# A two-layer decoder on one core: mLSTM output by token tile, a diagonal in the final norm, and sample steps and weight slabs in another order

## The chip, the cores and the metric

The kernel runs as one program on one core of a Trainium2 chip. The metric is the device time of one execution in microseconds (us), less is better; several executions are timed and their median is given. Beside these, one execution is recorded by the hardware profiler: its span, every instruction on every engine, what each engine waited for, and the clock that TensorE was granted. The engines are called as in the profile: PE (matrix products), PEld (its weight loads), DVE (vector engine), ACT (scalar engine), POOL (GpSimd), SP (the queue that issues most DMAs).

## What is computed

Two decoder layers work on 512 prompt tokens (one causal sequence) and 8 sample tokens (one step each, with states of their own). A layer adds to the residual a mix of three branches (mLSTM, gated linear attention, pooling), then a channel mixer: dense SwiGLU in layer 0, a top-2-of-8 mixture of experts in layer 1. A last RMS norm follows. The parts that matter here:

```python
# mLSTM, one head, prompt: b = cumsum(log f), m_t the running maximum
s   = (q_t . k_s) * exp(b_t - b_s + i_s - m_t)          # causal weights
num = sum_s s * v_s + w_inter * (C q_t)
den = sum_s s       + w_inter * (n . q_t)
h   = num / max(|den|, exp(-m_t))
C_new, n_new = decayed state + sum_s w_s v_s k_s^T, ... # state returned
# sample tokens: the same with one token and a state C0, n0, m0 of each
# gated linear attention: S_t = diag(a_t) S_{t-1} + k_t^T v_t ; o_t = q_t S_t
# head norm, gates, projections, experts ...
y = x * rsqrt(mean(x^2) + eps) * final_norm_g
```

The prompt starts from zero states, so its inter terms vanish. All is float32.

## The kernel before

Every engine has its own instruction stream, written out by hand, and semaphores order them. Activations stand feature-major (features on the 128 partitions, 520 tokens along the free axis). A weight slab is 128 x 1024 float32; ACT rounds it into `w_hi` (`split_hi`, L756), DVE takes the rest into `w_lo` (`split_lo`, L1132), and PE makes three products per tile (line 1847). A slab costs PE 48 of these matmuls.

The mixers of a layer are chains of small steps over several engines. To keep PE busy during them, the 48 projection slabs of the layer (q, k, v, pooling input, gates) are cut into 96 half slabs, and each engine's stream has calls `fill(k)` between its chain steps. On PE `fill` is k half slabs of products. On ACT every even half slab is a `split_hi` two slabs ahead. On DVE every even half slab (L1426) is a `split_lo` two slabs ahead and `fill_out` (L1440), which takes the result of the slab before from PSUM, so that PE may use that bank again. All engines count the same half slabs. Since each stream is strictly in order, a DVE that waits in a chain step also holds the splits queued behind it.

Order in a layer: `inputs`, `gla`, `gla_decode` (the 8 sample states of the gated linear attention, two groups `j`), `mlstm_columns`, `mlstm` (4 heads), `mlstm_decode` (8 sample states, 4 heads with two buffers), `head_norm`, gates and merge.

mLSTM, one head on PE (L1947): transposes of k and v and a broadcast of `row_M`, `fill(2)`, scores of key tiles 0 and 1, `fill(1)`, scores of 2 and 3, `fill(1)`, then the output group, `fill(2)`, a wait for `h`, the pooling products, `fill(1)`. The output group makes the numerator feature-major in PSUM bank 6 (`vt` as weights, `wgt` moving, 512 + 384 + 256 + 128 columns), the denominator in bank 7 on all partitions (`ones` as weights, the same columns), exp(-m) broadcast to bank 4 (`row_f`, 512 columns), the new state from `vw` and `kt`, and its `n` row. After the group ACT copies state and row out and takes the absolute value of the 128x512 denominator (L885), DVE takes the maximum with bank 4 (L1363), the reciprocal (L1365) and the product with the numerator (L1367, the step `h`), then does its `fill(3)`. The even halves fall so that in heads 0 and 2 the half slab that PE does right after the pooling products needs the first `fill_out` of this `fill(3)`; in heads 1 and 3 it doesn't.

POOL does the pooling averages (`pool_average`, L575), one per head, with elementwise instructions on 128x512 tiles, and issues the DMAs of states. After the last head it stores C, n and m, waits until these stores have landed (their memory is used again), loads the sample states and rows (`Cs`, `kb`, `qb`), waits for `sample_norms`, and sends its result through memory (`den_rows`) to all partitions (`rec_b`).

`mlstm_decode` on DVE (L1396): `fill(2)`, the same wait for the stores, `sample_norms` (L1371, nine steps on 8 partitions), then per head `Cs` times its factor, `kb` times its factor, `fill(2)`, their sum, the product with `qb`, `fill(2)`, a reduction and the product with `rec_b`. `gla_decode` on DVE (L1245): `fill(4)`, then the two products and the sum for group `j`, on which PE waits after a `fill(4)` of its own.

The end: after the last expert pass POOL stores the last outputs (`store_y`), waits for them in `stored` (L739: a wait on a register's value, a one-element POOL operation, a wait for that), and gathers each token's second row (`rows_back`, L726, five tiles). For each tile DVE adds it (L1784), ACT squares and sums and takes the root (L1084, L1087), DVE the reciprocal (L1789), ACT scales the 128x1024 tile (L1092), PE transposes it in 8 blocks (L2227) into one of two PSUM pairs, DVE multiplies by the gain (L1794), SP stores it.

Of the kernel before, what the change touches and what calls it, by code (L numbers as in the profile page):

```python
# [152 lines left out]
def decoder(nc, slabs, x_in, vectors, if_bias, gate_w, pool_w, consts, ml_m0, ml_n0, ml_C0,  # L153
# [7 lines left out]
    def sem(name):  # L161
# [54 lines left out]
    acol = sb("acol", [P, TT, H], where=early)  # L216
    w3 = sb("w3", [H, 3, NS_TOK], where=early)
# [34 lines left out]
    vt = sb("vt", [P, TT, P], where=ml_mem)  # L252
    wgt = sb("wgt", [P, TT, NP_TOK], where=ml_mem)
    dm = sb("dm", [P, TT, P], where=ml_mem)
    den = sb("den", [P, NP_TOK], where=ml_mem)
    den2 = sb("den2", [P, NP_TOK], where=ml_mem)
# [115 lines left out]

    rows = Steps(sem("rows"), gates=2, abs=2, exp=1, ln=1, logf=1, b=1, a=1, M=1, m=2, enm=1,
                 inter=1, smax=1, sdiff=3, sexp=1, turn=1, turned=4)
# [48 lines left out]
    second_in = [sem(f"second_in{i}") for i in range(5)]  # L423
    low_added, both_added = sem("low_added"), sem("both_added")
# [59 lines left out]

    def gathered_rest():

        return ps[:, 2:4, P:2 * P].rearrange("p a (b c) -> p a b c", c=REST)
# [9 lines left out]
    def pair(i):  # L497

        return 6 if i % 2 == 0 else 2

# [65 lines left out]
    def _(pool):  # L566
# [33 lines left out]
        for l in range(DEPTH):  # L600
# [33 lines left out]
            for h in range(H):  # L634
                pool_average(l, h)
                i = H * l + h
                pool.wait_ge(ml.sem, ml.after("cst", i))
                pool.dma_start(C_p[l, h], C_t[:, h]).then_inc(st_C, 16)
            pool.dma_start(n_p[l], n_row[:]).then_inc(st_nm, 16)
# [13 lines left out]
            for h in range(2):  # L653
# [3 lines left out]
            pool.wait_ge(sn.sem, sn.after("drec", l))  # L657
            pool.dma_start(den_rows[l, 0].rearrange("(b h) -> b h", h=H), den8[:, 2]).then_inc(den_stored, 16)
            pool.wait_ge(den_stored, 16 * (l + 1))
            pool.dma_start(rec_b[:].rearrange("p b h -> p (b h)"),  # L660
                           den_rows[l].to_broadcast([P, NS_TOK * H])).then_inc(rec_in, 16)
            pool.dma_start(n_s[l], n_s0[:]).then_inc(st_ns, 16)
# [56 lines left out]
        def store_y(j):  # L719

            pool.wait_ge(y_main, j + 2)
            pool.dma_start(slots[bass.ds(j * CAP, P)], yt[:, 0]).then_inc(y_stored, 16)
            pool.wait_ge(y_added, j + 2)
            pool.dma_start(slots[bass.ds(j * CAP + P, REST)], yt[0:REST, 1]).then_inc(y_stored, 16)
# [8 lines left out]
        with pool.Fori(0, last) as j:  # L733
            pool.wait_ge(gathered, j * 2 + 2)
            load_rows(j * CAP + CAP)
            store_y(j)
# [12 lines left out]
        store_y(last)  # L749
        stored(last * 32 + 48, 2)  # L750
# [4 lines left out]
    def _(act):  # L755
# [103 lines left out]
        def mlstm(l):  # L859
# [4 lines left out]
            for h in range(H):  # L864
# [20 lines left out]
                nc.scalar.activation(den[:], ps[:, 7], ACT.Abs).then_inc(ml.sem, 1)  # L885
# [192 lines left out]
        def last_norm():  # L1078

            for i in range(6):  # L1080
                if i < 5:
                    rws = slice(0, tile_rows(i))
                    act.wait_ge(both_added, i + 1)
                    nc.scalar.activation(rows_in[rws], xt[rws, i], ACT.Square,  # L1084
                                         accum_out=ssq[rws, i:i + 1]).then_inc(fin_sq, 1)
                    act.wait_ge(fin_sq, i + 1)
                    nc.scalar.activation(rst[rws, i:i + 1], ssq[rws, i:i + 1], ACT.Sqrt, bias=eps[rws],  # L1087
                                         scale=1.0 / D).then_inc(fin_root, 1)
                if i > 0:
                    rws = slice(0, tile_rows(i - 1))  # L1090
                    act.wait_ge(fin_rs, i)
                    nc.scalar.activation(xt[rws, i - 1], xt[rws, i - 1], ACT.Copy,  # L1092
                                         scale=rst[rws, i - 1:i]).then_inc(fin_scaled, 1)
# [33 lines left out]
    def _(dve):  # L1127
# [117 lines left out]
        def gla_decode(l):  # L1245

            for j in range(2):
# [5 lines left out]
                fill(4)  # L1253
# [5 lines left out]
                inc(tt_op(Ss[:, j], Ss[:, j], vb[:, j], ALU.add))  # L1259
                at("o")  # L1260
# [63 lines left out]
        def mlstm_columns(l):  # L1324
# [4 lines left out]
            inc(nc.vector.tensor_copy(acol[:], ps[:, 4, 0:16].rearrange("p (a h) -> p a h", h=H)))  # L1329
            inc(nc.vector.tensor_copy(w3t[:], ps[0:NS_TOK, 4, 32:44].rearrange("p (a h) -> p a h", h=H)))  # L1330
# [5 lines left out]
        def mlstm(l):  # L1336
            for h in range(H):
                rep = H * l + h
# [3 lines left out]
                inc(nc.vector.tensor_copy(vt[:], ps[:, 5].rearrange("p (a d) -> p a d", d=P)))  # L1342
# [17 lines left out]
                inc(tt_op(vw[:], vt[:], wcol[:].unsqueeze(2).to_broadcast([P, TT, P]), ALU.mult))  # L1360
# [35 lines left out]
        def mlstm_decode(l):  # L1396
# [3 lines left out]
            sample_norms(l)  # L1400
            for h in range(H):
# [10 lines left out]
                fill(2)  # L1412
# [357 lines left out]
        def last_norm():  # L1770
# [8 lines left out]
            for i in range(7):  # L1779
# [10 lines left out]
                if i > 1:  # L1790
                    rws = tile_rows(i - 2)
                    dve.wait_ge(fin_turned, i - 1)
                    b = pair(i - 2)
                    tt_op(x[:, :, P * (i - 2):P * (i - 2) + rws],  # L1794
# [41 lines left out]
    def _(pe):  # L1836
# [110 lines left out]
        def mlstm(l):  # L1947
# [21 lines left out]
            for h in range(H):  # L1969
                rep = H * l + h  # L1970
                at = lambda name: pe.wait_ge(ml.sem, ml.after(name, rep))
                if h > 0:
                    pe.wait_ge(po.sem, po.after(f"y{h - 1}", l))
# [392 lines left out]
```

## Time and profile before

| | us |
|---|---|
| median of 3 timed runs | 2181.29 (2179.46 to 2182.74) |
| the profiled execution, its own time | 2184.47 |
| its span, first to last instruction | 2182.8 |
| PE busy | 2073.6 (95%) |
| DVE busy | 1335.9 (61%) |
| ACT busy | 847.2 (39%) |
| POOL busy | 209.2 (10%) |

The time outside the span is 1.7 us. A row of a timeline has start, duration, engine, line, operation, output from inputs, shapes and count; in square brackets stands how long the engine was idle before it and what ended that.
### The profile page before, as it was taken

What the parts mean: (1) busy time and instruction counts of PE and PEld (TensorE: products, weight loads), DVE (VectorE), ACT (ScalarE), POOL (GpSimd) and SP (SyncE); (2) the same over time, 40 slices, a digit from 0 to 9 for tenths busy, and PEclk for the clock granted to TensorE, in tenths of its full rate; (3) what the DMA queues carried; (4) which work ended last, traced back from release to release, by engine and by line L of the source; (5) the groups of instructions that cost most, each with busy time, mean ns of one, the idle gap of its engine ahead of it and who ended that gap; (6) DMA issues with size and microseconds to landing.
All of it is one profiled execution on the core that took longest, in us unless ns stands there. A gap on an engine that the chain in (4) does not pass through costs nothing.

```text
span 2182.8 us, 38536 instructions
## 1 busy us (share of the span) xinstructions
PE 2073.6 (95%) x15443; PEld 1945.9 (89%) x15443; DVE 1335.9 (61%) x1964; ACT 847.2 (39%) x1175; POOL 209.2 (10%) x344
## 2 busy tenths in 40 slices
PE   7999999999999999999999999995999999999994
PEld 7998889999999999999988899994888888888873
DVE  5554457665555542345543666655788787888876
ACT  4311222543433222234122225433455555555644
POOL 0002231010000000000022310102000000000011
PEclk9999999999999999999999999997999999999996
DMA  4232238557222232222422384633677777787775
GB/s 177 81 116 84 91 103 283 171 180 282 93 89 96 87 97 93 92 88 79 119 86 79 128 278 151 189 99 120 214 241 243 239 249 247 225 262 238 241 263 165
DMA packets 108637, 352.37 MB, mean 161 GB/s; under 512 B 14168, under 2 KB 18328, under 8 KB 108248
## 3 DMA queue, kind: packets, MB, share of 16 engines
q1 hardware_dynamic: 87464, 278.46, 39.6%
q0 software_dynamic: 21056, 72.21, 10.0%
q8 instruction: 91, 1.49, 0.3%
q14 instruction: 26, 0.21, 0.0%
HBM read 304.80 MB, written 46.27 MB: 161 GB/s over the span
## 4 chain that ended last, share of the span: by engine, by line
PE 66%; DVE 14%; issue 7%; DMA 6%; ACT 6%; POOL 1%; ACTq 0%; SPq 0%; DVEq 0%; POOLq 0%
PE ps L1847 52%; PE ps L1841 7%; DVE w_lo L1135 6%; ACT w_hi L761 4%; DMA raw<-slabs 4%; PE ps L2151 3%; DVE gsum L1726 1%; PE ps L2153 1%; DVE usum L1737 1%; PE ps L2165 1%; DVE ma_parts L1767 1%; PE ps L2171 1%; DVE den L1365 1%; DVE yt L1762 0%; DMA mlstm_reciprocals<-den 0%
## 5 line engine op out<-in xcount | busy, mean ns | idle before, releaser
L1135 DVE TENSOR_TENSOR w_lo<-raw,w_hi 128x1024 fp32r<-128x1024 f32 x487 | 601.2, 1235 | 306.0 <-ACT w_hi L761 303.7
L761 ACT ACTIVATE w_hi<-raw 128x1024 fp32r<-128x1024 f32 x488 | 508.9, 1051 | 440.9 <-PE ps L1847 393.4
L1847 PE MATMUL ps<-h_hi,w_hi 128*128 128x260 f32 x2544 | 526.8, 288 | 21.7 <-DVE h_lo L1144 13.6
L1847 PE MATMUL ps<-h_hi,w_lo 128*128 128x260 f32 x2544 | 514.6, 284 | 0.0
L1847 PE MATMUL ps<-h_lo,w_hi 128*128 128x260 f32 x2544 | 513.9, 284 | 0.0
L1847 PEld LDWEIGHTS ps<-h_hi,w_hi 128*128 128x128 f32 x2544 | 396.9, 190 | 36.7 <-DVE w_lo L1135 22.0
L1847 PEld LDWEIGHTS ps<-h_hi,w_lo 128*128 128x128 f32 x2544 | 394.4, 189 | 0.0
L1847 PEld LDWEIGHTS ps<-h_lo,w_hi 128*128 128x128 f32 x2544 | 394.2, 190 | 0.0
L2151 PE MATMUL ps<-hg,w_hi 128*128 128x320 f32 x1408 | 375.3, 349 | 16.2 <-DVE w_lo L1135 12.9
L2153 PE MATMUL ps<-hg,w_lo 128*128 128x160 f32 x1408 | 334.8, 238 | 0.0
L2151 PEld LDWEIGHTS ps<-hg,w_hi 128*128 128x128 f32 x1408 | 266.2, 189 | 36.1 <-DVE w_lo L1135 24.0
L2153 PEld LDWEIGHTS ps<-hg,w_lo 128*128 128x128 f32 x1408 | 270.5, 192 | 2.0
L2165 PE MATMUL ps<-w_hi,ma_parts 128*128 128x512 f32 x352 | 115.5, 409 | 9.7 <-DVE w_lo L1135 9.0
L1056 ACT ACTIVATE msig<-gsum 128x160 f32<-128x160 f32 x88 | 29.5, 336 | 145.8 <-DVE gsum L1726 145.8
L2165 PEld LDWEIGHTS ps<-w_hi,ma_parts 128*128 128x128 f32 x352 | 59.3, 188 | 20.6 <-issue 10.7
L1847 PE MATMUL ps<-br_lo,w_hi 128*128 128x260 f32 x384 | 77.3, 283 | 0.0
L1847 PE MATMUL ps<-br_hi,w_hi 128*128 128x260 f32 x384 | 77.1, 282 | 0.0
L1847 PE MATMUL ps<-br_hi,w_lo 128*128 128x260 f32 x384 | 77.0, 282 | 0.0
L1847 PE MATMUL ps<-a_hi,w_hi 128*128 128x260 f32 x352 | 71.0, 283 | 0.0
L1847 PE MATMUL ps<-a_hi,w_lo 128*128 128x260 f32 x352 | 70.8, 282 | 0.0
L1847 PE MATMUL ps<-a_lo,w_hi 128*128 128x260 f32 x352 | 70.6, 282 | 0.0
L1064 ACT ACTIVATE ma_parts<-ma 128x160 fp32r<-128x160 f32 x88 | 29.7, 337 | 82.7 <-DVE ma L1739 82.4
(362 smaller groups left out, 2595.0 us busy)
## 6 DMA issues: line engine op xcount, KB each, us to landing
raw<-slabs SPq DMA_DIRECT2D x489, 512.0 KB, 4.2
gates_kept<-sq SPq DMA_DIRECT2D x64, 260.0 KB, 2.2
gs<-gates_kept POOLq DMA_DIRECT2D x64, 260.0 KB, 3.6
token_slots<-zeros POOLq DMA_DIRECT2D x1, 9600.0 KB, 34.7
rows_in<-token_slots POOLq DMA_DIRECT2D x9, 512.0 KB, 4.4
Cs<-ml_C POOLq DMA_DIRECT2D x8, 512.0 KB, 6.8
kb<-mlstm_key_query_rows POOLq DMA_DIRECT2D x8, 512.0 KB, 6.7
qb<-mlstm_key_query_rows POOLq DMA_DIRECT2D x8, 512.0 KB, 8.2
```

The lines of the kernel that those rows point to most:

```text
L761: nc.scalar.activation(w_hi[:, n % SPL], raw[:, place(n)], ACT.Copy).then_inc(hi_ready, 1)
L1056: nc.scalar.activation(msig[:], gsum[:], ACT.Sigmoid).then_inc(m_sig, 1)
L1064: nc.scalar.activation(ma_parts[:, f % 2, 0:CAP], ma[:, f % 2], ACT.Copy).then_inc(m_hi, 1)
L1135: tt_op(w_lo[:, n % SPL], raw[:, place(n)], w_hi[:, n % SPL].bitcast(F32), ALU.subtract).then_inc(lo_ready, 1)
L1365: inc(nc.vector.reciprocal(den2[:], den[:]))
L1726: nc.vector.tensor_reduce(gsum[:], addends(b), AX.X, ALU.add).then_inc(m_sum, 1)
L1737: nc.vector.tensor_reduce(usum[:], addends(b + 1), AX.X, ALU.add).then_inc(m_up, 1)
L1841: return mm(out, a, b, start=start, stop=stop, skip_group_check=True)
L1847: ins = mm(out[:, hf], wgt_part[:, slot, tile], in_part[:, kk, HALF * hf:HALF * (hf + 1)], start=first and not ends and in_part is in_hi, ...
L2151: mm(out[:, 0:2 * CAP], w_hi[:, (s0 + s) % SPL, kk], hg[:, kk], start=kk == 0, stop=False, skip_group_check=True)
L2153: ins = mm(out[:, 0:CAP], w_lo[:, (s0 + s) % SPL, kk], hg[:, kk, 0:CAP], start=False, stop=kk == KT - 1, skip_group_check=True)
L2165: mm(ps[:, 4 + hf_], parts[:, at:at + P], w[:, slot_n, 4 * hf_:4 * hf_ + 4], start=f == 0 and a == 0, stop=f == FE_TILES - 1 and a == 2)
```

## The change

Four edits:

- mLSTM output. `vt` has a 129th column of ones. For each query tile the weights `wgt` are the stationary operand and `vt` with its ones the moving one: 10 matmuls of 129 columns give numerator and denominator with tokens on partitions. The products with `ones` and the broadcast of `row_f` go; exp(-m) comes as columns (`fcol`) from four more small transposes before the heads. Absolute value, maximum and reciprocal are on 128x4; ACT scales each of the four query tiles into `out_rows`, PE transposes them back into bank 6 (the step `back`), DVE copies to `br`. On PE `back` stands where the wait for `h` was; the next head waits for `h`.
- Samples. `sample_norms` is called in the DVE stream ahead of head 1; POOL sends its result after head 1 and fetches it after head 2.
- Slabs. In `gla_decode` one slab of DVE's `fill` goes from ahead of each state to behind its sum; in `mlstm_decode` one goes from inside head 0 to ahead of it.
- The end. DVE makes a diagonal matrix of the reciprocal roots; PE multiplies each tile by it (float32 matmuls in place of transposes), so ACT's scaling goes; four PSUM pairs in place of two; DVE's product with the gain comes one turn later. The last stores have a semaphore of their own and are waited for directly.

```diff
     ml = Steps(sem("mlstm"), ...
-               vw=1, out=1, cst=2, absd=1, maxd=1, rec=1, h=1)
+               vw=1, out=1, cst=2, absd=1, maxd=1, rec=1,
+               scaled=TT, back=1, h=1)
 # POOL, head loop
                 pool.dma_start(C_p[l, h], C_t[:, h]).then_inc(st_C, 16)
+                if h == 1:
+                    pool.wait_ge(sn.sem, sn.after("drec", l))
+                    pool.dma_start(den_rows[l, 0]..., den8[:, 2]).then_inc(den_stored, 16)
+                    pool.dma_start(n_s[l], n_s0[:]).then_inc(st_ns, 16)
+                if h == 2:
+                    pool.wait_ge(den_stored, 16 * (l + 1))
+                    pool.dma_start(rec_b..., den_rows[l]...).then_inc(rec_in, 16)
 # POOL, end
-        store_y(last)
-        stored(last * 32 + 48, 2)
+        store_y(last, last_stored)
+        pool.wait_ge(last_stored, 32)
 # ACT, mlstm
-                nc.scalar.activation(den[:], ps[:, 7], ACT.Abs).then_inc(ml.sem, 1)
+                nc.scalar.activation(den[:]..., out_sums(), ACT.Abs).then_inc(ml.sem, 1)
+                at("rec")
+                for tt in range(TT):
+                    c = (P + 1) * (tt % 2)
+                    nc.scalar.activation(out_rows[:, tt], ps[:, 6 + tt // 2, c:c + P], ACT.Copy,
+                                         scale=den[:, tt:tt + 1]).then_inc(ml.sem, 1)
                 fill(2)
 # ACT, last_norm
-                    nc.scalar.activation(xt[rws, i - 1], xt[rws, i - 1], ACT.Copy,
-                                         scale=rst[rws, i - 1:i]).then_inc(fin_scaled, 1)
 # DVE, gla_decode
-                fill(4)
+                fill(2)
 ...
                 inc(tt_op(Ss[:, j], Ss[:, j], vb[:, j], ALU.add))
+                fill(2)
                 at("o")
 # DVE, mlstm
             for h in range(H):
+                if h == 1:
+                    sample_norms(l)
 ...
-                inc(tt_op(den[:], den[:], ps[:, 4], ALU.max))
+                inc(tt_op(den[:], den[:], fcol[:, :, h], ALU.max))
                 at("maxd")
-                inc(nc.vector.reciprocal(den2[:], den[:]))
-                at("rec")
-                inc(tt_op(br[:, h, 0:NP_TOK], ps[:, 6], den2[:], ALU.mult))
+                inc(nc.vector.reciprocal(den[:], den[:]))
+                at("back")
+                inc(nc.vector.tensor_copy(br[:, h, 0:NP_TOK], ps[:, 6]))
                 fill(3)
 # DVE, mlstm_decode
-            sample_norms(l)
+            fill(2)
 ...
                 inc(by_token(kb[:, b], vs8[:, h]))
-                fill(2)
+                if h > 0:
+                    fill(2)
 # DVE, last_norm
+                    dve.wait_ge(fin_rs, i)
+                    ts_op(root_diag(i - 1), ident[rws, rws], rst[rws, i - 1:i], None, ALU.mult).then_inc(
+                        fin_scaled, 1)
 # PE, mlstm
                 if h > 0:
                     pe.wait_ge(po.sem, po.after(f"y{h - 1}", l))
+                    pe.wait_ge(ml.sem, ml.after("h", rep - 1))
 ...
                 for tt in range(TT):
-                    exact(ps[:, 6, tt * P:], vt[:, tt], wgt[:, tt, tt * P:], tt == 0, tt == TT - 1)
-                for tt in range(TT):
-                    exact(ps[:, 7, tt * P:], ones, wgt[:, tt, tt * P:], tt == 0, tt == TT - 1)
-                exact(ps[:, 4], select[:, h], row_f[:, 0:NP_TOK])
+                    c = (P + 1) * (tt % 2)
+                    for ts in range(tt + 1):
+                        exact(ps[:, 6 + tt // 2, c:c + P + 1], wgt[:, ts, token_tile(tt)], vt[:, ts],
+                              ts == 0, ts == tt)
 ...
                 fill(2)
-                pe.wait_ge(ml.sem, ml.after("h", rep))
+                at("scaled")
+                for tt in range(TT):
+                    ins = nc.tensor.transpose(ps[:, 6, tt * P:(tt + 1) * P], out_rows[:, tt], ident)
+                ins.then_inc(ml.sem, 1)
 # PE, end
-            if i >= 2:
-                pe.wait_ge(fin_out, i - 1)
+            if i == 4:
+                pe.wait_ge(fin_out, 1)
             for kk in range(KT):
-                ins = nc.tensor.transpose(ps[:, pair(i) + kk // 4, ...], xt[...], ident[...])
+                ins = exact(ps[:, tail_pair(i) + kk // 4, ...], xt[...], root_diag(i))
```

## Rows read from the trace of the kernel before

**Rows 1.** The page, busy time of each engine over the span.
```profile
PE 2073.6 (95%) x15443; PEld 1945.9 (89%) x15443; DVE 1335.9 (61%) x1964; ACT 847.2 (39%) x1175; POOL 209.2 (10%) x344
```

**Rows 2.** Waits of PE, whole span: who waited for whom, total, times, longest.
```profile
PE ps L1847 <- DVE sq L1450: 6.7, 7, 2.1
PE ps L1841 <- DVE Ss L1259: 3.5, 4, 0.9
```

**Rows 3.** Timeline of PE in mLSTM head 0 of layer 0.
```profile
199.61 2.32 PE L1841 MATMUL ps<-wgt,vt 128*128 128x512 f32 x8
...
205.07 1.16 PE L1841 MATMUL ps<-kt,vw 128*128 128x128 f32 x8
...
207.12 0.51 PE L1847 MATMUL ps<-h_hi,w_hi 128*128 128x260 f32 x2
...
213.17 1.15 PE L1841 MATMUL ps<-pd,pw 128*128 128x260 f32 x4
215.00 0.47 PE L1847 MATMUL ps<-h_hi,w_hi 128*128 128x260 f32 x2 [0.69 <-DVE sq L1450]
```

**Rows 4.** Timeline of PE in the gated linear attention: matmuls of 128 columns.
```profile
136.73 0.39 PE L1841 MATMUL ps<-qz,S_in 128*128 128x128 f32 x2
136.95 0.39 PE L1841 MATMUL ps<-att,gvt 128*128 128x128 f32 x2
```

**Rows 5.** Timeline of ACT after the output group of head 0.
```profile
207.23 0.28 ACT L881 ACTIVATE C_t<-ps 128x128 f32<-128x128 f32 x1 [14.18 <-PE ps L1841]
```

**Rows 6.** Timeline of DVE, end of head 0 and begin of head 1, layer 0.
```profile
209.04 3.35 DVE L1365 RECIPROCAL den<-den 128x512 f32<-128x512 f32 x1
213.03 1.21 DVE L1135 TENSOR_TENSOR w_lo<-raw,w_hi 128x1024 fp32r<-128x1024 f32 x1
...
216.03 2.42 DVE L1135 TENSOR_TENSOR w_lo<-raw,w_hi 128x1024 fp32r<-128x1024 f32 x1 [1.17 <-ACT w_hi L761]
...
220.16 0.69 DVE L1342 COPY vt<-ps 128x512 f32<-128x512 f32 x1 [1.11 <-PE ps L1841]
...
224.01 0.17 DVE L1347 COPY wcol<-wgt 128x4 f32<-128x4 f32 x1 [2.43 <-ACT wgt L877]
```

**Rows 7.** Timeline of POOL at the begin of head 1, layer 0.
```profile
216.30 1.05 POOL L581 TENSOR_TENSOR pa<-br 128x511 f32<-128x511 f32 x1
217.41 1.07 POOL L582 COPY pa<-br 128x1 f32<-128x1 f32 x1
```

**Rows 8.** Timeline of DVE, begin of `mlstm_decode` in layer 0.
```profile
321.69 0.18 DVE L1377 TENSOR_TENSOR vs<-v,w3b 128x32 f32<-128x32 f32 x1
...
325.78 0.17 DVE L1394 RECIPROCAL den<-den 8x4 f32<-8x4 f32 x1
...
329.18 1.23 DVE L1266 TENSOR_TENSOR kb<-kb,vs 128x1024 f32<-128x1024 f32 x1
```

**Rows 9.** Busy time of engines by stretch, then PEclk, DMA share, GB/s.
```profile
1077.00:1078.00 1.00, 1.00 (x6) 1.00 (x6) 0.85 (x2) 0.00 (x0) 0.42 (x1) 0.50 0.02 8
```

**Rows 10.** Busy time of PE in a stretch of the routing, then PEclk.
```profile
1498.00:1498.50 0.50, 0.50 (x5) 0.50 0.00 0
```

**Rows 11.** Timeline of PE in the routing.
```profile
1495.85 4.49 PE L2106 MATMUL ps<-con,x 128*128 128x128 f32 x24
```

**Rows 12.** Timeline of POOL at the end: the wait for the last stores.
```profile
2151.85 1.86 POOL L742 TENSOR_TENSOR rst<-rst 1x1 f32<-1x1 f32 x1 [1.75 <-DMA token_slots<-yt]
2154.31 1.45 POOL L729 DMA_INDIRECT second<-token_slots,order  x1 [0.60 <-POOL rst L742]
```

**Rows 13.** Timeline of PE at the end.
```profile
2165.30 1.97 PE L2227 MATMUL ps<-con,xt 128*128 128x128 f32 x8 [21.34 <-ACT xt L1092]
```

**Rows 14.** Timeline of DVE at the end.
```profile
2161.41 1.28 DVE L1784 SCALAR_TENSOR_TENSOR xt<-second,share,xt 128x1024 f32<-128x1024 f32 x1 [1.05 <-DMA second<-token_slots,order]
...
2176.74 1.39 DVE L1794 TENSOR_TENSOR x<-ps,vec 128x1024 f32<-128x1024 f32 x2 [1.12 <-PE ps L2227]
```

**Rows 15.** One line's instructions: count, duration min, median, max.
```profile
L1229 DVE TENSOR_SCALAR S_in<-S,ge x16: 276/278/283, 105.9 to 1055.7; 128x128 f32<-128x128 f32 x16
```

More of the change, by code:

```diff
@@ L216, in decoder @@
     acol = sb("acol", [P, TT, H], where=early)
+    fcol = sb("fcol", [P, TT, H], where=early)
     w3 = sb("w3", [H, 3, NS_TOK], where=early)
@@ L251, in decoder @@
     kt = sb("kt", [P, TT, P], where=ml_mem)
-    vt = sb("vt", [P, TT, P], where=ml_mem)
+    vt = sb("vt", [P, TT, P + 1], where=ml_mem)
     wgt = sb("wgt", [P, TT, NP_TOK], where=ml_mem)
     dm = sb("dm", [P, TT, P], where=ml_mem)
-    den = sb("den", [P, NP_TOK], where=ml_mem)
-    den2 = sb("den2", [P, NP_TOK], where=ml_mem)
+    out_rows = sb("out_rows", [P, TT, P], where=ml_mem)
+    den = sb("den", [P, TT], where=ml_mem)
+    sb("beside_den", [P, NP_TOK - 4 * TT], where=ml_mem)
     vw = sb("vw", [P, TT, P], where=ml_mem)
@@ L499, in pair, with tail_pair, root_diag @@
         return 6 if i % 2 == 0 else 2
+    def tail_pair(i):
+        return (6, 2, 4, 0)[i % 4]
+    def root_diag(i):
+        return gain_row[0:tile_rows(i), P * i:P * i + tile_rows(i)]
     def gain_of(r):
@@ L656, in _ @@
                 across(qb, 1, h, qb_in)
[L657 to L662, printed above, removed]
             for h in range(H):
@@ L735, in _ @@
             load_rows(j * CAP + CAP)
-            store_y(j)
+            store_y(j, y_stored)
         pool.wait_ge(gathered, last * 2 + 2)
@@ L1078, in last_norm @@
         def last_norm():
[L1080 to L1091, printed above, removed]
-                    nc.scalar.activation(xt[rws, i - 1], xt[rws, i - 1], ACT.Copy,
-                                         scale=rst[rws, i - 1:i]).then_inc(fin_scaled, 1)
+            for i in range(5):
+                rws = slice(0, tile_rows(i))
+                act.wait_ge(both_added, i + 1)
+                nc.scalar.activation(rows_in[rws], xt[rws, i], ACT.Square,
+                                     accum_out=ssq[rws, i:i + 1]).then_inc(fin_sq, 1)
+                act.wait_ge(fin_sq, i + 1)
+                nc.scalar.activation(rst[rws, i:i + 1], ssq[rws, i:i + 1], ACT.Sqrt, bias=eps[rws],
+                                     scale=1.0 / D).then_inc(fin_root, 1)
         fills = [0, 0]
@@ L1329, in mlstm_columns @@
             inc(nc.vector.tensor_copy(acol[:], ps[:, 4, 0:16].rearrange("p (a h) -> p a h", h=H)))
+            inc(nc.vector.tensor_copy(fcol[:], ps[:, 4, 64:80].rearrange("p (a h) -> p a h", h=H)))
+            nc.vector.memset(vt[:, :, P:P + 1], 1.0).then_inc(ones_beside, 1)
             inc(nc.vector.tensor_copy(w3t[:], ps[0:NS_TOK, 4, 32:44].rearrange("p (a h) -> p a h", h=H)))
@@ L1778, in last_norm @@
                        ALU.add).then_inc(low_added, 1)
-            for i in range(7):
+            for i in range(8):
                 if i < 5:
@@ L1953, in mlstm @@
                                     ident[0:H, 0:H])
+                nc.tensor.transpose(ps[:, 4, 64 + H * tt:64 + H * tt + H], row_f[:, token_tile(tt)],
+                                    ident[0:H, 0:H])
             for a in range(3):
@@ L1973, in mlstm @@
                     pe.wait_ge(po.sem, po.after(f"y{h - 1}", l))
+                    pe.wait_ge(ml.sem, ml.after("h", rep - 1))
+                else:
+                    pe.wait_ge(ones_beside, l + 1)
                 for tt in range(TT):
@@ L2223, in _ @@
             pe.wait_ge(fin_scaled, i + 1)
-            if i >= 2:
-                pe.wait_ge(fin_out, i - 1)
+            if i == 4:
+                pe.wait_ge(fin_out, 1)
             for kk in range(KT):
-                ins = nc.tensor.transpose(ps[:, pair(i) + kk // 4, P * (kk % 4):P * (kk % 4) + rws],
-                                          xt[0:rws, i, P * kk:P * (kk + 1)], ident[0:rws, 0:rws])
+                ins = exact(ps[:, tail_pair(i) + kk // 4, P * (kk % 4):P * (kk % 4) + rws],
+                            xt[0:rws, i, P * kk:P * (kk + 1)], root_diag(i))
             ins.then_inc(fin_turned, 1)
```

31 lines of the change are left out of this document (20 added, 11 removed).

## The prediction

> **What bounds it now.** I read the busy times first: PE works 95% of the span [rows 1], so time is saved where PE gets less to do or where PE waits, and nowhere else. Then the waits of PE. Two of them are touched: PE waits 7 times, 6.7 us in all, for the DVE product that frees a PSUM bank (`fill_out`), and 4 times, 3.5 us, for the sum of a sample state in `gla_decode` [rows 2]. Of the 6.7, four are the 0.69 us after the pooling products in heads 0 and 2 of each layer [rows 3]; the other 3.9 lie in `mlstm_decode`. The timelines of one head (PE, ACT, DVE, POOL) show the rest: the output group runs from 199.61 to 207.12, its first three products until 205.07, so 5.46 us; the `fill(2)` behind it until about 213.1; and the reciprocal of 3.35 us [rows 6] ends with its neighbours just as this fill does, so it costs PE nothing today. Last, the end: PE idles 21.3 us and begins at 2165.30 [rows 13].
>
> **mLSTM heads.** The three products of 5.46 us become 10 matmuls of 128 by 129. Their price is not in the trace for this operand pair; the nearest rows are the 128-column matmuls of the gated attention, one start each 0.22 us [rows 4], and the four of the state, 1.16 us with their drain, 0.29 each [rows 3]. So 2.2 to 2.9 us, and the gain is 2.6 to 3.2 us; I take 2.9. Against it stand four transposes. The blocks of 8 in the routing give 4.49/24 = 0.19 us with the clock partly at half [rows 11]; I take 0.11 at the full clock, 0.45 us for four. The chain between, ACT's copies and absolute value, two tiny DVE steps and four scalings of some 0.28 us [rows 5], ends about 2.6 us after the group and is hidden by the 6 us of `fill(2)`; without this fill it would cost those 2.6 us. What is late next: DVE now waits for `back`, and its `fill(3)` is queued behind. Let F be the end of PE's `fill(2)`. Today DVE begins the split at 213.03 and PE starts its next half slab at 215.00, F + 1.9 [rows 3, 6]. Then: transposes to F + 0.65, DVE copy 0.6, and the same 1.97 from split to PE: F + 3.2. Heads 0 and 2 lose 1.3 us, heads 1 and 3, whose next half slab needs nothing of this, 0.5. Gain per layer 2 x (2.9 - 1.3) + 2 x (2.9 - 0.5) = 8.0; both layers 16.0 (13.6 to 18.4). The four small transposes, `fcol` and the column of ones ahead of the heads cost PE about 0.3 us per layer, an estimate below one 128-column matmul each [rows 4]: -0.6.
>
> **Sample norms ahead of head 1.** Nine DVE steps last from 321.69 to 325.95, 4.3 us [rows 8]. In the old place they stood before the load of `kb` had landed (329.18) and were nearly free. In the new place DVE comes out of head 0 at F + 6.5 (after the split that took 2.42 us in place of 1.21 [rows 6]), so the steps end at F + 10.8 if nothing disturbs them. Queued behind them is the `vt` copy, which PE's transposes allow at F + 8.1. From that copy to the `wcol` that PE waits for are 4.05 us [rows 6]; PE's own `fill(2)` covers until F + 14.0. So PE waits at least 0.85 us. But POOL begins its pooling average just here. The rows show both sides blocking: the split that doubled ran into POOL's addition, and POOL's one-column copy took 1.07 us while the split ran [rows 6, 7]. The six norm steps with two SBUF inputs that are long or early may each wait for one POOL step of 0.2 to 1.5 us, which puts the end at F + 14.7 and the wait at 4.7 us. The Trainium skill (SBUF - State Buffer, Who interferes with whom) states that a DVE instruction with two SBUF inputs and a POOL instruction that reads SBUF exclude each other for a whole instruction, while a reduction does not contend. Without such a lock the loss would be 0.85 us a layer, with it 4.7. By these rows [rows 6, 7] I take 4.0. A PE that idles 4 us then finds its clock at half; the trace has three such stretches after idle time or tiny matmuls, one of them at 1077 [rows 9] lasting from 1076 to 1083, the others (332 and 1304) about 3 to 4 us; at half the clock that is 1.5 us lost. Sum 2 x 5.5 = -11.0, bounds -1.7 to -13.
>
> **Slabs and decode.** With `rec_b` ready and one slab ahead, DVE no longer has a split queued behind the `kb` transfer (landed 329.18), and the 3.9 us of PE waits go. What is next is PE itself: two slabs of 5.8 us per head against 9.8 us of DVE work; the loads of the third and fourth state come just in time. +3.9, bounds 1 to 3.9. In `gla_decode` the sum comes one split and one `fill_out` (1.8 us) sooner, more than the 0.9 of each wait; only group 0 is bound by its transfer. Of 3.5 I take 2.8 (2.0 to 3.5). Two of the half-clock stretches, 1076 and 332, follow waits that go; they cost about 3.4 and 1.4 us. Such stretches can fall elsewhere, so I take half, 2.4 (0 to 4.8).
>
> **The end.** The one-element POOL operation takes 1.86 us and the gather starts 0.6 later, at 2154.31 [rows 12]. The direct wait gives back 1.2 (gathers then run beside DVE's additions) to 2.4; I take 1.7. Tile 0's scale is then ready after DVE's second addition (2161.41 + 1.2 - 1.7), a reciprocal and a diagonal of 0.28 us [rows 14, 15]: PE starts at 2161.5 in place of 2165.30. Its price rises: a tile took 1.97 us [rows 13], and 8 matmuls take 1.8 to 2.3 us at the full clock, 3.5 to 4.6 at half. The clock is at half after 21 us of idling. In the routing PE is busy without a gap with transposes alone while its clock stands at half [rows 10, 11]; before, it never rose in the end either. The Trainium skill (TensorE: Matmul & The Clock Gate, Part 4: PE-mode transpose) says that transposes do not count as busy for the clock; the trace agrees [rows 10, 11]. By that the new matmuls would raise it, and an end of transposes would stay at half. From 1076 and 332 it took 3 to 7 us of matmuls. With the rise inside tile 1 the tiles end at 2165.5, 2168.5, 2170.6 and 2172.8; with the product behind, DVE is done at 2174.2 in place of 2178.1 [rows 14]: +3.9. With a full clock throughout +5.4, at half throughout -3.1.
>
> **The sum.** 16.0 - 0.6 - 11.0 + 3.9 + 2.8 + 2.4 + 3.9 = 17.4 us. The durations are of the profiled execution (2184.5, span 2182.8), which is 3.2 us above the median of 2181.3; as nearly all terms are differences inside it, I take them off the median: 2163.9, say 2164.
>
> **The rivals.** 1. The norms run undisturbed beside POOL, lose 0.85 us a layer and no clock: 9.3 us better, 2154.6; with the other terms at their good ends 2148. For it: many of the steps are short, and POOL pauses between its own. Against: the blocking shown above [rows 6, 7]. Chance 0.22. 2. The clock stays at half at the end: 7.0 us worse, 2171. For it: the bursts are short and wait for each other; chance 0.14. 3. The moved slabs bring nothing, because the state transfers and not the order set the decode stages: 3.9, 2.8 and 2.4 go, 2173. For it: DVE waits there for `Cs` and `kb` after the norms; against: the waiting DVE is the one with PE's splits queued behind it. Chance 0.10. 4. Slower than before: each 129-column matmul pays twice the 0.22 to 0.29 us, as it would at the half clock or with weight loads that aren't hidden. At 0.55 us the ten cost 5.5, the group gains nothing, and the sum falls by 8 x 2.9 = 23.2: 2187. It decides from 0.47 us per matmul (0.256 + 17.4/80). Against: both near rows are below 0.3. Chance 0.04. The forecast itself has 0.48, between 2157 and 2169; 0.02 stays for a change that moves nothing.
>
> **Range and chances.** From 2150 (most of rival 1) to 2174 (rivals 2 and 3). A measurement of this kernel tells about 0.2%, 4.4 us, from no change. Faster than 2177: the forecast and rivals 1 to 3 but for their worst overlap, 0.91; within 0.2%: 0.05; slower: 0.04.
>
> **What would show it.** In the profile after: ten `wgt`/`vt` matmuls of 128x129 in 2.2 to 2.9 us; PE waits of about 2 us for `fill_out` after the pooling products in heads 0 and 2, none in 1 and 3; a PE wait for `wcol`'s successors at the scores of head 1, 0.9 to 4.7 us long, with the norm steps stretched between POOL's steps; no PE wait for `Ss` and none for `fill_out` in the decode; a gather at about 2.0 us after the last store landed, and a clock that rises in the second tile of the end. The forecast is wrong if the head period does not shrink by 1.6 and 2.4 us, or if head 1 loses more than 6 us a layer.

## The result, and the profile after

| | before | after |
|---|---|---|
| median of 4 timed runs each, us | 2180.38 (2177.34 to 2182.74) | 2147.31 (2145.57 to 2149.66) |
| ratio of after to before, 95% interval | | 0.985 [0.9833, 0.9867] |
| the profiled execution: span, us | 2182.8 | 2145.6 |
| mean granted clock of its span | 0.981 | 0.986 |

The change gains 33 us. The forecast was 17.4 us, and 2147.3 lies below the low end of its range, 2150: right in sign, half the size. The busy times of after, against [rows 1]:

```profile
PE 2045.9 (95%) x15539; PEld 1942.3 (91%) x15539; DVE 1307.6 (61%) x1973; ACT 847.3 (39%) x1202; POOL 209.1 (10%) x343
```

PE is still the bound; its busy time is 27.7 us shorter, what it lost at half clock included. The waits of PE (who waited for whom, total, times, longest), to be read against [rows 2]:

```profile
PE ps L1869 <- DVE gain_row L1816: 17.0, 1, 17.0
PE ps L1875 <- DVE sq L1475: 11.2, 7, 2.1
PE ps L1869 <- DVE wcol L1371: 1.5, 1, 1.5
```

The waits for `Ss` are gone. Those for the DVE product have grown from 6.7 to 11.2 us: four of 1.74 us are the stall in heads 0 and 2, 0.69 us before [rows 3], and three, of 0.65, 1.46 and 2.12 us, lie in `mlstm_decode`. The wait that I priced highest, that for `wcol` (a small copy of DVE ahead of the scores) at head 1, is there once, with 1.5 us. PE in head 0 of layer 0, to be read against [rows 3]: the ten matmuls and what follows them, the four transposes, the pooling products and the stall.

```profile
197.73 2.40 PE L1869 MATMUL ps<-vt,wgt 128*128 128x129 f32 x20
199.97 1.06 PE L1869 MATMUL ps<-kt,vw 128*128 128x128 f32 x8
...
207.77 0.60 PE L2039 MATMUL ps<-con,out_rows 128*128 128x128 f32 x4
208.21 1.04 PE L1869 MATMUL ps<-pd,pw 128*128 128x260 f32 x4
210.99 0.48 PE L1875 MATMUL ps<-h_hi,w_hi 128*128 128x260 f32 x2 [1.74 <-DVE sq L1475]
```

To see where the 37.2 us between the two spans went, I took from both timelines of PE the starts of the same instructions, stage by stage. The last column is what the sum of the prediction says for the stage.

| stage | layer 0 gain, us | layer 1 gain, us | both | forecast |
|---|---|---|---|---|
| gated attention, `gla_decode`, columns | 2.05 | 5.11 | 7.2 | 3.9 |
| mLSTM heads, first `row_M` product to the last pooling product | 8.35 | 10.12 | 18.5 | 5.0 |
| `mlstm_decode`, from there to `head_norm` | 1.27 | 0.02 | 1.3 | 4.6 |
| `head_norm` to the merge | 0.00 | 3.19 | 3.2 | 0 |
| experts, which no edit touches | | | 2.8 | 0 |
| end, from the issue of the last store | | | 4.4 | 3.9 |

(3.9 = 2.8 - 0.6 + 1.7 for half of the clock stretch at 1076; 5.0 = 16.0 - 11.0; 4.6 = 3.9 + 0.7 for half of that at 332.) The profiled execution of before is 4.1 us above its median, that of after is at its median; so about as much of the two rows with nothing in the forecast, 6.0 us, belongs to this one execution of before. The stage from `head_norm` to the merge shows it: in layer 1 it took 19.8 us there, with a wait of 2.44 us and a stretch at half clock, but 16.6 in after and 16.9 in the run with the end alone, which changes nothing in this stage.

### The profile page after: what moved, and what is told of

The parts are those of the page before. It is cut to its first block, busy times and chain, and to the rows that moved or that the text cites. A ratio compares the mean times of both kernels' runs of the same rounds, so it can differ in the third digit from the quotient of the medians.

```text
span 2145.6 us, 38756 instructions
## 1 busy us (share of the span) xinstructions
PE 2045.9 (95%) x15539; PEld 1942.3 (91%) x15539; DVE 1307.6 (61%) x1973; ACT 847.3 (39%) x1202; POOL 209.1 (10%) x343
## 4 chain that ended last, share of the span: by engine, by line
PE 70%; DVE 11%; DMA 7%; issue 6%; ACT 5%; POOL 1%; ACTq 0%; SPq 0%; DVEq 0%; POOLq 0%
PE ps L1875 53%; PE ps L1869 6%; DVE w_lo L1154 5%; PE ps L2186 5%; ACT w_hi L781 3%; DMA raw<-slabs 3%; PE ps L2200 2%; PE ps L2188 2%; PE ps L2206 1%; DVE gsum L1751 1%; DVE usum L1762 1%; DMA C_s<-Cs 1%; DMA Cs<-ml_C 1%; DVE ma_parts L1792 1%; DVE yt L1787 0%
## 5 line engine op out<-in xcount | busy, mean ns | idle before, releaser
L2200 PEld LDWEIGHTS ps<-w_hi,ma_parts 128*128 128x128 f32 x352 | 59.3, 188 | 21.2 <-issue 10.9
```

Of the source, the lines that this page charges most:

```text
L2200: mm(ps[:, 4 + hf_], parts[:, at:at + P], w[:, slot_n, 4 * hf_:4 * hf_ + 4], start=f == 0 and a == 0, stop=f == FE_TILES - 1 and a == 2)
```

## The experiments

The first four take one part of the change each, on the kernel before (the slab of `mlstm_decode` goes with the norms); the others start from the changed kernel. In all of them the kernel before ran on the same chip, and ratios are to that.

**The mLSTM output alone.** Its edits are the hunks on `vt`, `fcol`, `out_rows`, `den` and the step `back`.

> The kernel before with the mLSTM output edit alone (tokens on partitions, the 129th column, the transposes back); norms, slabs, gla_decode and the end as before. Theory A, from the stage marks of the two traces: the head periods shrink by 2.1 us (heads 0, 2) and 3.0 us (heads 1, 3), 20 us in all, less 0.6 for the columns: 2161 (2159 to 2164), with no PE wait at the scores of head 1. Theory B, the sizes of the forecast (16.0 less 0.6): 2165. If much of the 33 us were not of this edit but of the others, the time lies above 2166.

2165.1 us, ratio 0.9932 [0.9916, 0.9948]. Theory A's number is missed, B's is met, but not for B's reason. The heads gain what A says: their periods are 32.05, 30.03, 31.99 and 25.36 us for 34.11, 33.19, 34.13 and 28.41 in layer 0, 10.4 us a layer. What the time lacks is lost elsewhere: `mlstm_decode` is longer by 1.3 and 2.4 us, and this execution has six stretches at half clock in the mixers, where that of before has three. Timeline of PE and granted clock (the number before the DMA share) around the two products of `gla_decode` in layer 0:

```profile
153.85 1.95 PE L1856 MATMUL ps<-qz,Ss 128*128 128x2 f32 x16 [0.84 <-DVE Ss L1272]
156.00:159.00 3.00, 3.00 (x16) 0.50 0.52 179
172.00:176.00 4.00, 4.00 (x23) 0.60 0.55 184
```

**The norms, and the slab of `mlstm_decode`, alone.**

> The kernel before with the sample norms behind the first head and the slab ahead of the state in mlstm_decode, nothing else. Theory A (DVE keeps going beside POOL's average, POOL is the one that is delayed): the norms take 5 to 6 us there, PE waits 1 to 2.5 us at the scores of head 1 in each layer, the decode gives back 1 to 4: 2180 (2177 to 2183). Theory B (each norm step waits for a POOL step, and the idle PE loses its clock, as forecast): 11.0 lost, 3.9 won, 2187.5.

2179.0 us, ratio 1.0003 [0.9991, 1.0014]: theory A. PE waits 2.56 us in layer 0 and 0.94 in layer 1 at the scores of head 1; heads 1 and 2 together are 3.1 and 1.3 us longer in the two layers, and the decode is 3.4 and 1.1 us shorter. By itself this edit moves nothing that can be measured; the forecast gave it -7.1.

**`gla_decode` alone.**

```diff
-                fill(4)
+                fill(2)
                 dve.wait_ge(S_in_s[j], 16 * (l + 1))
...
                 inc(tt_op(Ss[:, j], Ss[:, j], vb[:, j], ALU.add))
+                fill(2)
```

> The kernel before with the slab moved behind the sum in gla_decode alone. Theory A, from the stage marks of the two traces: the four waits of PE for the state's sum (3.5 us) go, and with them the half-clock stretch at 1076 to 1083 of layer 1: 2173 (2172 to 2176). Theory B: only the waits go, the clock falls elsewhere: 2177.5. Theory C: the state transfer sets this stage: 2180.

2169.7 us, ratio 0.9958 [0.9941, 0.9975], below theory A's range: the stage gains 2.3 us in layer 0 and 5.4 in layer 1, as A says, and this execution has no stretch at half clock anywhere in the mixers. The rows that answer to those above (PE's product, then the granted clock behind it):

```profile
152.64 1.84 PE L1842 MATMUL ps<-qz,Ss 128*128 128x2 f32 x16
155.00:159.00 4.00, 4.00 (x35) 1.00 0.77 273
170.00:174.00 4.00, 4.00 (x39) 1.00 0.91 284
```

The product has no wait in front, and the clock stays. Over all profiles of this case, one of each kernel: in the four kernels with the old order the 16 products have a wait of 0.84 to 0.94 us in front, and 10 of them are followed by a fall; in the ten with the new order none of the 40 is.

**The end alone.**

> The kernel before with the end alone changed (diagonal as the moving operand, own semaphore of the last stores). Theory A: from the issue of the last store to the end 28.8 us in place of 33.2, so 2176 (2175 to 2177). Theory B: the 4.4 us are in part of the stages ahead of it, 2178 to 2180.

2176.2 us, ratio 0.9985 [0.9974, 0.9996]: theory A. From the issue of the last store to the end of the span it takes 28.7 us, as in after (28.8; before 33.2).

**The norms back in their old place**, with the old order of the slabs in `mlstm_decode`.

> The changed kernel with the sample norms and the slab order of mlstm_decode as they were before; the rest stays changed. Theory A (the norms cost PE only the 1.5 us seen at head 1 of layer 0, and the decode is set by its state transfers): heads 1.5 faster, decode 1 to 4 slower, 2147 to 2151, about no change. Theory B (the sizes of the forecast): 11.0 won, 3.9 lost, 2140.

2150.4 us, ratio 0.9852 [0.9835, 0.9869], for 0.985 of the changed kernel: theory A. Heads 1 and 2 together gain 2.1 us in layer 0 and 0.3 in layer 1, the decode loses 1.0 and 2.6 us. Both single-edit runs agree: the norms' place is worth about nothing in sum, and not -7.

**The norms twice**, ahead of head 1.

```diff
                 if h == 1:
-                    sample_norms(l)
+                    sample_norms(l, sn2)
+                    dve.wait_ge(sn2.sem, sn2.after("drec", l))
+                    sample_norms(l, sn)
```

> The changed kernel with the nine steps of the sample norms done twice in a row ahead of head 1 (the second time on the results of the first, so the samples' part of the output is another). Theory A (the place has no cover left: 1.5 us of wait in layer 0, a margin of 0.1 in layer 1): every further us of DVE there is a us of PE, 4.3 to 5.6 per layer, so 2157 (2155.5 to 2160), the upper end if the idle PE also falls to the half clock. Theory B (PE's cover is longer than the wait in layer 0 lets it look): under 2152.

2160.4 us, ratio 0.99 [0.9885, 0.9916], 13.1 us more than the changed kernel by the medians and 11 by the ratios: theory A, at its upper end. The waits of PE at the scores of head 1, layers 0 and 1, and the clock in the first:

```profile
227.92 2.07 PE L1872 MATMUL ps<-q,k 128*128 128x512 f32 x2 [5.82 <-DVE wcol L1374]
1145.18 2.08 PE L1872 MATMUL ps<-q,k 128*128 128x512 f32 x2 [5.22 <-DVE wcol L1374]
226.00:234.00 8.00, 6.08 (x19) 0.57 0.31 97
```

So the place has no cover left beyond the first nine steps: nine more cost PE 4.3 and 5.2 us, and after these longer waits the clock falls, which adds some 2.9 and 1.6 us. The mechanism of the forecast exists; one set of norms doesn't reach it.

**One half slab ahead of the transposes back.**

```diff
                 inc(nc.vector.reciprocal(den[:], den[:]))
+                fill(1)
                 at("back")
                 inc(nc.vector.tensor_copy(br[:, h, 0:NP_TOK], ps[:, 6]))
-                fill(3)
+                fill(2)
```

> The changed kernel with one half slab of DVE's fill moved from behind the copy of the transposed output to ahead of its wait. Theory A: PE's four waits of 1.74 us behind the pooling products in heads 0 and 2 were the split queued behind that wait; they go, and the 1.5 us at head 1 of layer 0 with them: 2139 (2138 to 2142). Theory B: what is next on DVE or ACT (w_hi) is as late as the split was, the time stays above 2145.

2145.2 us, ratio 0.9833 [0.982, 0.9847], against 0.985 [0.9833, 0.9867] of the changed kernel, so no gain clear of the noise. Theory A's 2139 is missed; B's "above 2145" is met, barely, and its reason in part. The four stalls are gone, as A says (heads 0 and 2 take 30.0 to 30.3 us), but head 1 takes them back: 35.3 and 33.8 us for 31.8 and 30.2. The waits there:

```profile
223.64 2.05 PE L1870 MATMUL ps<-q,k 128*128 128x512 f32 x4 [3.49 <-DVE wcol L1371]
1131.70 2.17 PE L1870 MATMUL ps<-q,k 128*128 128x512 f32 x4 [1.91 <-DVE wcol L1371]
```

PE arrives 2.0 us earlier; DVE does not, since its second split waits 1.86 us for `w_hi` of ACT, as B has it, and the norms end at 219.7, where in the changed kernel they end at 219.5. The gain is turned into a longer wait for the norms, with a half-clock stretch behind it in each layer.

**The states of heads 2 and 3 in a buffer of their own.** All four states are loaded at once.

```diff
+            for h in range(2):
+                pool.dma_start(Cs2[:, h], ml_C0[l, h + 2]).then_inc(C2_in[h], 16)
             for h in range(H):
...
-                    pool.wait_ge(st_Cs, 16 * (i + 1))
-                    pool.dma_start(Cs[:, h % 2], ml_C0[l, h + 2]).then_inc(C_in[h % 2], 16)
```

> The changed kernel with the sample states of heads 2 and 3 in a buffer of their own (the keys' tile, which nobody reads by then), so that they are loaded with those of heads 0 and 1 and wait for no store. Theory A (the chain store of head 0, load of head 2 in the same buffer sets mlstm_decode): DVE's idle 3.9 and 4.6 us for Cs go, and PE's waits of 0.65, 1.46 and 2.12 us: 2143.5 (2142 to 2145). Theory B: kb and qb, which still wait for the head, come as late: 2146 to 2148.

2144.6 us, ratio 0.9834 [0.982, 0.9848]: theory A by its number, though the medians alone don't set it apart from the changed kernel; the stage does. The decode takes 55.65 and 56.35 us for 58.24 and 58.02. First the chain in the changed kernel, layer 0 (POOL's store of head 0, POOL's load for head 2 into the same buffer, DVE's first step of head 2), then that step with the own buffer:

```profile
327.72 0.54 POOL L686 DMA_DIRECT2D C_s<-Cs  x1 [12.16 <-DVE br L1449]
333.37 0.53 POOL L691 DMA_DIRECT2D Cs<-ml_C  x1 [4.08 <-DMA C_s<-Cs]
340.98 1.23 DVE L1286 TENSOR_TENSOR Cs<-Cs,w3b 128x1024 f32<-128x1024 f32 x1 [3.94 <-DMA Cs<-ml_C]
```

```profile
336.17 1.23 DVE L1288 TENSOR_TENSOR k<-k,w3b 128x1024 f32<-128x1024 f32 x1
```

Head 0 is done at 327.4; the store and the load keep the buffer until 341.0. With the state in the keys' tile DVE goes from head 1 to head 2 without a pause. What is left of the 1.46 and 2.12 us waits of PE is one of 0.46 us.

**The norms in a gap of DVE.** In head 1 DVE has nothing to do from the reciprocal to the transposes back, 5.4 us, and POOL is idle then.

```diff
-                if h == 1:
-                    sample_norms(l)
                 rep = H * l + h
...
                 inc(nc.vector.reciprocal(den[:], den[:]))
+                if h == 1:
+                    sample_norms(l)
                 at("back")
```

> The changed kernel with the sample norms moved from ahead of head 1 into head 1, behind the reciprocal, where DVE idles 5.4 us until the transposes back and POOL has nothing to do; POOL sends and fetches their result one head later. Theory A (the norms cost PE what DVE's queue at the begin of head 1 makes them cost): they take 4.3 us as in the old place, PE has no wait at the scores of head 1, the periods of head 1 are 30.0 us in both layers in place of 31.8 and 30.2: 2145 (2143 to 2147). Theory B: they delay the copy behind the transposes, and head 2 is as much longer: 2147.

2143.4 us, ratio 0.9837 [0.9812, 0.9862]: theory A. Head 1 takes 30.03 us in both layers, and there is no wait for `wcol`. This run is also the measure for what the norms and POOL do to each other. The norms on DVE in the changed kernel, beside POOL's average:

```profile
213.90 0.67 DVE L1401 TENSOR_TENSOR vs<-v,w3b 128x32 f32<-128x32 f32 x1
214.49 0.67 DVE L1403 TENSOR_TENSOR kq<-kq,w3t 8x512 f32<-8x512 f32 x1
215.27 0.68 DVE L1406 TENSOR_TENSOR n_s<-n_s,w3t 8x512 f32<-8x512 f32 x1
215.98 0.98 DVE L1408 TENSOR_TENSOR n_s<-n_s,kq 8x512 f32<-8x512 f32 x1
217.00 0.68 DVE L1410 TENSOR_TENSOR kq<-kq,n_s 8x512 f32<-8x512 f32 x1
217.71 0.67 DVE L1412 TENSOR_REDUCE den<-kq 8x4 f32<-8x512 f32 x1
218.42 0.73 DVE L1414 SCALAR_TENSOR_TENSOR den<-den 8x4 f32<-8x4 f32 x1
219.18 0.15 DVE L1416 TENSOR_TENSOR den<-den,w3t 8x4 f32<-8x4 f32 x1
219.37 0.17 DVE L1418 RECIPROCAL den<-den 8x4 f32<-8x4 f32 x1
```

The three of them that are longer with POOL at work, as they are with the norms in the gap:

```profile
234.90 0.16 DVE L1401 TENSOR_TENSOR vs<-v,w3b 128x32 f32<-128x32 f32 x1
...
236.47 0.68 DVE L1408 TENSOR_TENSOR n_s<-n_s,kq 8x512 f32<-8x512 f32 x1
...
238.61 0.15 DVE L1414 SCALAR_TENSOR_TENSOR den<-den 8x4 f32<-8x4 f32 x1
```

And the same steps of POOL's average at the begin of head 1, first in the changed kernel with the norms beside them, then with the norms in the gap:

```profile
213.49 1.03 POOL L598 TENSOR_TENSOR pa<-pa 128x510 f32<-128x510 f32 x1
214.59 0.63 POOL L599 COPY pa<-pa 128x2 f32<-128x2 f32 x1
215.31 2.00 POOL L603 TENSOR_SCALAR pd<-pa 128x512 f32<-128x512 f32 x1
...
217.84 1.30 POOL L605 TENSOR_TENSOR pd<-pd,br 128x512 f32<-128x512 f32 x1
```

```profile
214.54 0.19 POOL L599 COPY pa<-pa 128x2 f32<-128x2 f32 x1
214.82 1.49 POOL L603 TENSOR_SCALAR pd<-pa 128x512 f32<-128x512 f32 x1
```

In layer 0 DVE loses 0.5, 0.3 and 0.6 us on three steps, 1.4 in all, and POOL loses 0.4 and 0.5; in layer 1 DVE loses 0.3 and 0.7 us on two. Both wait, each a part of the time.

**Two, then three edits together.** The norms in the gap and the half slab ahead of the transposes; then the buffer of the states as well.

> The changed kernel with the norms in the gap of head 1 and one half slab of the fill ahead of the transposes back. Theory A (the half slab alone only moved the wait to the norms at head 1): heads 0, 1 and 2 take 30.0 us each in both layers, 10.2 us less than in the changed kernel's profile: 2137 (2135 to 2140). Theory B (DVE or ACT have no room for it): head 1 or the decode takes back 3 us or more, 2140 to 2144.

2135.6 us, ratio 0.9798 [0.9773, 0.9822]: theory A. Heads 0 to 2 take 30.0 us each in both layers, and PE waits for nothing in the heads. With the norms out of the way, the half slab gives 7.8 us more; alone its 2.1 us were within the noise. The time of the heads in the profiles says the same: 8.0 us less here, 1.0 less there.

> The same with the states of heads 2 and 3 in a buffer of their own. Theory A: the 10.2 us of the heads, and the 2.6 and 1.7 us of the decode that this buffer gave alone: 2133 (2131 to 2136). Theory B: the heads come earlier, the states don't, and the decode waits for them: 2136 to 2139.

2132.2 us, ratio 0.9783 [0.9759, 0.9807]: theory A, 15 us below the changed kernel and 48 below the one before. The page and the waits of PE for DVE's products:

```profile
PE 2045.0 (96%) x15539; PEld 1943.5 (91%) x15539; DVE 1306.3 (61%) x1973; ACT 847.7 (40%) x1202; POOL 207.7 (10%) x343
```

```profile
PE ps L1878 <- DVE sq L1478: 1.8, 2, 0.9
```

PE is busy for the same 2045 us as in after; the gain is waits alone, 11.2 us of them now 1.8, and none for `wcol`.

**The old scaling at the end**, with the own semaphore kept.

> The changed kernel with the scaling of the last tiles by ACT and PE's transposes as before; the own semaphore of the last stores stays. Theory A: the gather still starts 2.8 us after the issue of the last store, PE starts 1.5 us later than in the changed kernel, its clock stays at half through the tiles, and they take 17.5 us to the end in place of 16.6: 2149.8 (2149 to 2151.5). Theory B: the clock rises with the transposes too, and the tiles end earlier: 2147 to 2148.5.

2149.3 us, ratio 0.9862 [0.9834, 0.9891]: theory A's time, and theory B's clock. POOL's first gather starts 2.8 us after the issue of the last store, as in after; before it was 4.7 (issued at 2149.57, gather at 2154.31 [rows 12]). The same two rows in after:

```profile
2116.80 0.53 POOL L744 DMA_DIRECT2D token_slots<-yt  x1 [1.50 <-DVE yt L1787]
2119.56 2.09 POOL L749 DMA_INDIRECT second<-token_slots,order  x1 [2.24 <-DMA token_slots<-yt]
```

With the old scaling PE starts 11.4 us after the gather, for 9.5 with the diagonal, and from there it takes 17.1 us to the end, for 16.6. So of the 4.4 us at the end 2.0 are the semaphore's and 2.4 the diagonal's. The clock, though, doesn't stay at half (stretch, its length, PE's busy time, granted clock, DMA share, GB/s):

```profile
2129.00:2132.00 3.00, 2.53 (x11) 0.50 0.00 0
2132.00:2133.00 1.00, 1.00 (x7) 0.63 0.00 0
2133.00:2136.00 3.00, 0.14 (x2) 1.00 0.62 184
2137.00:2139.00 2.00, 1.52 (x8) 0.50 0.33 95
```

PE has run nothing but transposes since 2129.0, and the clock is at 1.00 from 2133 on, while PE waits for the next tile; then it falls again, and with more transposes alone it is back at 1.00 from 2139.6 to 2143.0.

## Why the prediction was wrong

**The step that failed: the sample norms, -11.0.** The order of events was right. The `vt` copy stands behind the norms, PE's cover ends at the scores of head 1, and the wait is put down to `wcol`. The price was not. I let the six norm steps with two inputs wait for POOL, up to 1.5 us each, and took a PE wait of 4.0 us near that upper end; they last 5.6 and 5.2 us in place of 4.3, and PE waits 1.5 and 0 us. Compared with the heads without the norms, heads 1 and 2 are 2.1 and 0.3 us longer, 2.4 in all. This is 8.6 us of the miss. Rival 1, to which I gave 0.22, has the price nearly right (0.85 us a layer, no clock), though the norms were not undisturbed, as it says. Whether PE waits at all in layer 1 goes with the split just ahead of the norms: in after it took 1.23 us there and PE did not wait; in the run with the states apart, which has the same code here, the split ran into POOL's addition and took 2.64 us, and PE waited 1.76. The rows of before [rows 6, 7] showed each engine delayed once by the other. I read this as DVE waiting at every step, though the row of POOL's copy, 1.07 us for one column, showed POOL waiting as well. The Trainium skill (SBUF — State Buffer, Who interferes with whom) has the two excluding each other for a whole instruction, whoever issues first going ahead, and reductions free of it. The trace agrees beside POOL's additions: L1401 ends 0.05 us after that of 213.49, L1414 0.01 us after that of 217.84, and the reduction takes 0.67 us in both places. It differs beside POOL's TENSOR_SCALAR of 215.31 to 217.31: L1408 begins and ends inside it and is longer by 0.30 us only, and there the measurement decides. So neither does DVE wait at every step nor is each wait a whole POOL step; the price of 4.0 us had both. The 1.5 us of half clock per layer fell with the wait: in after no stretch at half follows it. Doubling the norms, with waits of 5.8 and 5.2 us, brought both back.

**The heads: right in mechanism, too small in size.** 16.0 was forecast, 20.9 is what the edit gives. The ten matmuls take 2.24 us from 197.73 to 199.97, the low end of 2.2 to 2.9, while I took 2.56: 0.3 us in each of 8 heads. Heads 0 and 2 lose 1.1 us to the stall in place of 1.3, heads 1 and 3 almost nothing in place of 0.5: the transposes cost PE 0.44 us, but state group and pooling product follow 0.1 to 0.2 us closer on their neighbours. The rival with 129 columns at double price did not occur.

**`gla_decode`: too small.** The waits, with the products and half slabs around them, give 2.3 us per layer, 4.6 for the 2.8 forecast; I had charged it for group 0, which in after has no wait either. The stretch at half clock I counted to one half. The runs show that it goes with its cause: with a wait before the tiny products the clock fell in 10 of 16 cases, without it in none of 40. The small transposes ahead of the heads cost 0.2 to 0.3 us a layer, as forecast.

**The decode: the term was right, and another edit took it away.** Between the heads alone and the changed kernel the decode gains 2.6 and 2.4 us, 5.0 for the 3.9 forecast. But the new heads cost it 1.3 and 2.4 us first, a half-clock stretch in each layer included where before has one in layer 0: PE's waits there grow from 2.07 and 1.66 us to 3.49 and 2.98. Their last part, from head 3 to its pooling product, is 3.05 us shorter, while POOL's chain behind the last head (stores, landing of `m_s`, loads) is not: the first state's load is issued 7.3 us after the last pooling product in before and 8.1 with the heads alone. My sentence that the third and fourth state come just in time was wrong: store and load in one buffer are late by 3.94 us. So in after PE still waits three times for `fill_out` in the decode, where I expected no wait. There rival 3 held: the transfers set this stage, and the own buffer shows it. (Single executions differ here: the same decode took 58.2 and 58.0 us in after, 57.2 and 59.3 in the run with the old scaling.) In `gla_decode` rival 3 did not hold.

**The end: right in size**, 4.4 for 3.9, by both of its parts (2.0 for 1.7, 2.4 for 2.2). PE starts at 2129.05, 9.5 us after the gather, and the clock:

```profile
2129.00:2135.00 6.00, 5.95 (x28) 0.50 0.05 16
2135.00:2141.00 6.00, 6.00 (x54) 0.99 0.76 222
```

It rises at the end of the second tile, as assumed, so rival 2 is out. The reason that I gave for it is wrong: by the Trainium skill (TensorE: Matmul & The Clock Gate, Part 4: PE-mode transpose) an end of transposes would stay at half, and the old scaling above reached 1.00 after transposes alone. There rule and measurement differ, and the measurement decides. The trace of before says so too, and I misread it: the 24 transposes of [rows 11] run to 1500.34, and a microsecond after the stretch of [rows 10], at 1499.5, the clock rises under them (stretch, its length, busy time of PE, PEld, DVE, ACT and POOL, granted clock, DMA share, GB/s):

```profile
1498.00:1499.00 1.00, 1.00 (x7) 1.00 (x6) 0.90 (x5) 0.64 (x1) 0.06 (x2) 0.50 0.00 0
1499.00:1500.00 1.00, 1.00 (x9) 0.66 (x7) 1.00 (x1) 0.68 (x1) 0.69 (x3) 0.74 0.00 0
1500.00:1501.00 1.00, 0.34 (x4) 0.04 (x1) 0.68 (x2) 0.98 (x2) 0.99 (x1) 1.00 0.02 0
```

In after PE has no gap between the tiles until the clock is up and none behind; with the transposes it waits 2.9 us before the third tile, and the clock falls again. Whether the gap alone does this was not tried.

**The sum again**: 8.6 (norms) + 4.9 (heads) + 3.3 (attention, with its clock) - 3.3 (decode) + 0.5 (end) = 14.0 us more than 17.4. This is 31.4 of the 33.1 measured; the rest lies in the last stretch at half clock and the experts, less what the profiled execution of before has above its median. The four edits alone add up to 26.6 us of medians (0.68, -0.03, 0.42 and 0.15%); 6 us are missing. Each of these medians is uncertain by 2 to 4 us, so this gap is not clear of the noise; that the edits help each other fits it, but is not shown: the heads alone keep the clock falls that the new `gla_decode` removes, and the decode loss that the slabs make good.

## What to carry to other kernels

A moved piece costs the bound engine only what its queue is longer than the cover: price the piece undisturbed first, add the delays that rows show one by one, and keep a lock at every step as the bound, not as the value. When one stage gets shorter, look at the transfers that start behind it at a fixed distance. And before a gain is counted, ask what is queued next: the half slab alone gave nothing clear of the noise, and 8 us once the norms stood in a gap where neither DVE nor POOL had work.

## What the runs showed of the hardware

A short wait of PE can cost more than its length. A wait of 0.84 to 0.94 us ahead of tiny products was followed, in 10 of 16 cases, by a stretch at half clock of 3 to 7 us, 1.7 to 3.4 us lost. Among the full matmuls of the mixers, the waits of 5.82, 5.22, 3.49 and 3.13 us were followed by such a stretch, the four of 1.74 us in the changed kernel were not, and of those between both kinds were seen: 1.78, 1.91 and 2.07 us with a stretch behind them, 1.93, 2.12 and 2.56 us without. So between 1.7 and 2.6 us the length of the wait alone does not tell. In the mixers the profile of before has three such stretches, that of after none; 6.8 us of the difference between these two executions are this; not all of it is the change's, since the one at 1305 is in no other profile. And transposes, which the prediction took to leave the clock at half, were alone on PE when it rose to 1.00 in the run with the old scaling.
